# The first four weight units of a two-layer encoder: the order in which halves of the channels are multiplied, loaded and split

## The chip, the cores and the metric

The kernel runs on one core of one Trainium2 chip. The metric is the device time of the whole kernel in microseconds (us), lower is better. The engines are called PE (matrix multiply), DVE (vector), ACT (scalar), POOL (general purpose) and SP (which here only issues transfers).

## The reference

Two layers over a sequence of 256 tokens with 1024 channels. Each layer normalises x, multiplies it by one wide matrix W_in, feeds the columns of the product to three branches (grouped-query attention A, dilated window attention B, pooling C) and to gates, and ends with a SwiGLU mixer.

```python
for l in range(DEPTH):                       # DEPTH = 2
    h = rms_norm(x, norm_mix[l])             # x: 256 x 1024
    z = h @ w_in[l]                          # 1024 x 6656, 13 chunks of 512 columns
    qa, ka, va, qb, kb, vb, uc, gz = jnp.split(z, SPLIT_POINTS, axis=-1)
    qa = apply_axial_rope(rms_norm(qa...), ang_row, ang_col)
    ...
    x = x + merged @ w_out[l]
    h2 = rms_norm(x, norm_ffn[l])
    x = x + (jax.nn.silu(h2 @ w_ffn_gate[l]) * (h2 @ w_ffn_up[l])) @ w_ffn_down[l]
```

## The kernel before, in words

**Units.** All weights of a layer lie in the order of their use as 68 units of 128 x 2048 floats (1 MB): four tiles `k` of 128 channels by 512 output columns. A chunk z0 to z12 of W_in takes two units, one for each half of the channels. Before the change unit `t` holds chunk `t // 2`, half `t % 2`. Four slots (`RING`) hold the units; SP loads the next unit into a slot when PE has finished the one in it (`unit_done`).

**Products in three parts.** Products are made nearly exact by splitting both factors into a rounded part and a rest. For each unit ACT writes `w_hi`, a rounded copy of `w_raw` (L658, `split`), and DVE writes `w_lo = w_raw - w_hi` (L854). PE then runs, for each of the two token blocks m = 0, 1, the eight matmuls hi x hi and lo x hi of the four tiles (L1135, L1137) and the four with `w_lo` (L1146): 24 matmuls of 512 columns a unit. The first unit of a layer is split in four pieces, one for each tile (L654, L860), and in the first layer it is also loaded in four pieces.

**Turning x.** PE needs x with channels on the partitions. A "turn" `("mix_x", i)` is four transposes of 128 x 128 (L1168) of half `i // 2` of the channels and token block `i % 2` into a bank; DVE multiplies by the gains into `scratch` (L878), ACT writes the rounded part `aT_hi` (L670), and DVE the rest `aT_lo` (L887). Turns 0 and 1 are made ahead of a layer's first unit. Turns 2 and 3 are listed in `TURNS_WITHIN` at unit 0: PE transposes them between the eight `w_hi` matmuls and the four `w_lo` matmuls of block m = 0 (`TURNS_FIRST`). The norm itself is applied later: ACT squares x into sums (`x_squares`, L761), POOL turns the sums into `rstd` (`x_norms`), and ACT applies `rstd` when it takes a finished chunk out of its bank (`take_z`, L755 and L756).

**Programs.** Every engine has its own program, one stretch for each unit `t`, in which the order is written out by hand. ACT splits up to three units ahead in the first two stretches (`splits_at(t, ahead=3)`), DVE two. At the start of both layers ACT's order is: first unit, (first layer: turns,) units 1 and 2, (second layer: turns,) squares of both halves of x, unit 3, then z0. Once z0 is taken, DVE normalises and rotates heads (`rotate`, L929 to L953, then `norm_rotated`, L961) in stretches named in `REGIONS`, ACT cuts the heads into 16-bit halves (L730), SP transposes them by a transfer, and ACT joins them (`join_heads`, L736). The first scores (L1225) start ahead of unit 10 and wait for the join of region a_k. DVE's maximum over the scores is L967.

**Banks.** z0, z2 and z4 lie in banks 2 and 3, all other chunks of W_in in banks 0 and 1. So z6's first matmul of block 0, at unit 12, waits until ACT has taken block 0 of z5 (finished at unit 11).

**Start of the kernel.** SP issues, in this order: x's first half for m = 0, piece 0 of the first unit, x's first half for m = 1, pieces 1 to 3, x's second half (512 KB), units 1, 2 and 3. POOL issues its own loads (gains, rotary table, mask, biases) once x's second half has landed. PE runs warm-up matmuls (L1267) before and after the first two turns.

Of the kernel before, what the change touches and what calls it, by code (L numbers as in the profile page):

```python
# [16 lines left out]
F32 = mybir.dt.float32  # L17
# [3 lines left out]
ALU = mybir.AluOpType  # L21
# [3 lines left out]
P = 128  # L25
# [48 lines left out]
    ("a_q", QK_A_Q, 8, 0, 0, 0, (2, 3)),  # L74
    ("a_k", QK_A_K, 2, 8, 1, 1, (4, 4)),
# [8 lines left out]
JOINS_AHEAD = {8: [(1, 0), (1, 1)], 13: [(3, 0)]}  # L84
JOINS_BEHIND = {7: [(0, 0)], 10: [(0, 1)], 14: [(2, 0)], 15: [(4, 0)], 16: [(4, 1), (5, 0)], 17: [(3, 1)],
# [24 lines left out]
    0: [("mix_x", 2), ("mix_x", 3)],  # L110
# [8 lines left out]
TURNS_FIRST = (0, U_A1, U_OUT + 3, U_FFN)  # L119
# [24 lines left out]
def turns_within(t):  # L144
    return TURNS_WITHIN.get(t, [])
# [50 lines left out]
UNIT_ENDS = {(f"z{c}", 1): 2 * c + 1 for c in range(Z_CHUNKS)}  # L196
# [20 lines left out]
def splits_at(t, ahead=2):  # L217

    if t < 2:
        return {2: ([1], [2, 3]), 3: ([1, 2], [3])}[ahead][t]  # L220
    return [t + 2] if t + 2 < UNITS else []


def build(nc, x, stream, params, b_gate, eye, angles, pooling, mask, out):
# [3 lines left out]
    with ExitStack() as ctx:  # L228
# [3 lines left out]
        def sem(name):  # L232
            return ctx.enter_context(nc.semaphore(name))
# [86 lines left out]
        unit_landed = [sem(f"unit_landed{i}") for i in range(RING)]  # L320
        piece_landed = [sem(f"piece_landed{k}") for k in range(UK)]
# [67 lines left out]
        def wait_lo(eng, lay, name, former=False):  # L389

            n = SCALED_TURNS.index(name) + 1 + EARLY_TURNS - (len(SCALED_TURNS) if former else 0)
            eng.wait_ge(turn_lo, lay * len(SCALED_TURNS) + n)

# [71 lines left out]
        def _(sp):  # L465
# [8 lines left out]
            sp.sem_inc(unit_landed[0], 16)  # L474
            sp.dma_start(x_sb[:, :, NC:D], xv[:, :, NC:D]).then_inc(x1_loaded, 16)
# [165 lines left out]
        def _(act):  # L641
# [5 lines left out]
            def split_first(lay):  # L647

                if lay:
                    act.wait_ge(unit_landed[0], lay * (16 * UNITS // RING) + 16)  # L650
                for k in range(UK):
                    if lay == 0:
                        act.wait_ge(piece_landed[k], 16)
                    nc.scalar.activation(w_hi[:, 0, k, :], w_raw[:, 0, k, :], ACT.Copy).then_inc(first_hi, 1)  # L654
# [108 lines left out]


            act.wait_ge(half_ready, 1)
# [3 lines left out]
            turn(BEFORE, ("mix_x", 0))  # L769
            for lay in range(DEPTH):  # L770
                for t in range(UNITS):
                    for name in turns_before(t, lay):
                        turn(lay, name)
                    if t == 0:
                        split_first(lay)
                        if lay == 0:
                            turn(BEFORE, ("mix_x", 1))
                            for name in turns_within(t):
                                turn(lay, name)
                    for j in splits_at(t, ahead=3):  # L780
# [27 lines left out]
                    if t or lay:  # L808
                        for name in turns_within(t):
                            turn(lay, name)  # L810
                    if t == 0:
                        for half in range(2):
                            for m in range(MT):

                                b = X_BANKS[half] + m
                                act.wait_ge(bank_free[b], lay * USES[b] + 1)
                                if half == 1:
                                    act.wait_ge(x1_loaded, 16)
                                x_squares(lay, m, half)
                    if t % 2 == 1 and t // 2 <= POOL_CHUNK:  # L820
                        for m in range(MT):
                            if (t, m) != FIRST_OUT:
                                take_z(lay, t // 2, m)
# [15 lines left out]
        def _(dve):  # L839
# [11 lines left out]
            def split(lay, j):  # L851
                dve.wait_ge(unit_hi, lay * (UNITS - 1) + j)
# [3 lines left out]
            def split_first(lay):  # L856

                for k in range(UK):
                    dve.wait_ge(first_hi, lay * UK + (k + 1))
                    nc.vector.tensor_tensor(w_lo[:, 0, k, :], w_raw[:, 0, k, :], w_hi[:, 0, k, :].bitcast(F32),  # L860
                                            ALU.subtract).then_inc(first_lo, 1)
# [174 lines left out]
            for lay in range(DEPTH):  # L1036
# [3 lines left out]
                for t in range(UNITS):  # L1040
# [7 lines left out]
                    if t == 0:  # L1048
                        split_first(lay)
                        if lay == 0:  # L1050
                            low_turn(BEFORE, ("mix_x", 1))
# [66 lines left out]
        def _(pe):  # L1118
            pe.sem_inc(unit_done, RING)

            def rows(lay, t, name, m, src, tiles, wk, first, final, opening=False, ready=None):
# [8 lines left out]
                if opening and t:  # L1130
                    pe.wait_ge(unit_hi, lay * (UNITS - 1) + t)
                for i, k in enumerate(tiles):
                    if opening and not t:
                        pe.wait_ge(first_hi, lay * UK + (i + 1))
# [6 lines left out]
                if opening and t:  # L1141
                    pe.wait_ge(unit_lo, lay * (UNITS - 1) + t)
                for i, k in enumerate(tiles):
                    if opening and not t:
                        pe.wait_ge(first_lo, lay * UK + (i + 1))
                    last = nc.tensor.matmul(o, src[0][:, k, tok], w_lo[:, slot, wk + i, :], start=False,  # L1146
                                            stop=final and i == len(tiles) - 1)
                if final:
                    full(last, (name, m))
                return last  # L1150
# [127 lines left out]
            for lay in range(DEPTH):  # L1278
                for t in range(UNITS):
# [10 lines left out]
                    if t < U_C0:  # L1290
                        c, half = divmod(t, 2)
                        ready = (lambda m: wait_lo(pe, lay, ("mix_x", 2 * half + m), former=half == 0)) if c == 0 else None
# [81 lines left out]
def weight_stream(w_in, w_branch_a, w_branch_b, w_branch_c, w_out, w_ffn_gate, w_ffn_up, w_ffn_down):  # L1374
# [3 lines left out]
    for l in range(DEPTH):  # L1378
        u = units[l]
        w = w_in[l].reshape(2, UK, P, Z_CHUNKS, NC)  # L1380
        u[:U_C0] = w.transpose(3, 0, 2, 1, 4).reshape(2 * Z_CHUNKS, P, UK, NC)
        c = w_branch_c[l].reshape(UK, P, 2, NC)
# [55 lines left out]
```

## Time and profile before

| | |
|---|---|
| median of 3 runs | 810.91 us (810.03 to 812.22) |
| the profiled execution's own time | 810.14 us |
| its span, first to last instruction | 808.3 us |
| PE busy | 802.1 us, 3808 matmuls |
| DVE, ACT, POOL busy | 572.9, 464.0, 245.9 us |
| clock that PE was granted | full in every slice |

The span is what the trace covers; 1.84 us of the profiled execution's time lie around it. An engine's busy time says how much of the span it worked, not that it was waited for: a matmul's listed duration (0.39 us) is longer than the distance at which the next one starts (0.227 us), because matmuls overlap, so distances between starts are the better measure of PE.

### The profile page before, as it was taken

Reading aid. Unit: us, or ns where it says so; the run is one execution under the profiler, and the core shown is the slowest. Engines: PE = TensorE matmul, PEld = TensorE weight load, DVE = VectorE, ACT = ScalarE, POOL = GpSimd, SP = SyncE. Lnnn points to the kernel's source line nnn. Section 1 sums busy time; section 2 is a strip of 40 time slices with the busy share of each in tenths; the row PEclk is TensorE's granted clock in tenths of the full one; section 3 lists DMA queues with packets and bytes.
Section 4 is the critical chain, followed back from the end, with each engine's and each line's share of the span. In section 5 each row is a group of like instructions: output and inputs, shape, how many; then the busy total and the mean of one; then the engine's idle time right before and its main releaser. Section 6 shows DMA issues by size and latency. Waiting matters only on the chain.

```text
span 808.3 us, 9803 instructions
## 1 busy us (share of the span) xinstructions
PE 802.1 (99%) x3808; PEld 658.5 (81%) x3808; DVE 572.9 (71%) x684; ACT 464.0 (57%) x534; POOL 245.9 (30%) x206
## 2 busy tenths in 40 slices
PE   8999999999999999999999999999999999999998
PEld 6888877888888888888888887878888888888886
DVE  5899976758685666665379998777686666676551
ACT  5788886574355445544457888856635455355420
POOL 1342623330043444430023325342300444344200
PEclk9999999999999999999999999999999999999999
DMA  9788876864557787686456888675744666776651
GB/s 336 285 242 217 216 225 216 215 223 161 171 211 210 212 220 218 202 244 217 163 203 201 223 226 215 214 222 190 234 156 167 222 207 208 231 234 201 206 205 53
DMA packets 98318, 170.22 MB, mean 211 GB/s; under 512 B 78016, under 2 KB 78176, under 8 KB 80864
## 3 DMA queue, kind: packets, MB, share of 16 engines
q1 hardware_dynamic: 96352, 163.34, 65.5%
q0 software_dynamic: 1632, 6.18, 2.2%
q8 instruction: 30, 0.49, 0.2%
q14 instruction: 16, 0.13, 0.1%
q10 hardware_dynamic: 288, 0.08, 0.0%
HBM read 149.91 MB, written 1.05 MB: 187 GB/s over the span
## 4 chain that ended last, share of the span: by engine, by line
PE 97%; DVE 1%; DMA 1%; ACT 0%; SPq 0%; issue 0%
PE bank L1135 31%; PE bank L1146 30%; PE bank L1137 30%; PE bank L1257 2%; PE bank L1168 1%; PE bank L1234 1%; PE bank L1225 1%; PE bank L1195 1%; DMA x_sb<-in_x_dram 1%; PE bank L1201 0%; DVE w_lo L854 0%; DVE w_lo L860 0%; ACT w_hi L658 0%; DVE scratch L878 0%; DVE aT_lo L887 0%; ACT aT_hi L670 0%
## 5 line engine op out<-in xcount | busy, mean ns | idle before, releaser
L854 DVE TENSOR_TENSOR w_lo<-w_raw,w_hi 128x2048 fp32r<-128x2048 f32 x134 | 314.6, 2349 | 122.5 <-ACT w_hi L658 121.9
L658 ACT ACTIVATE w_hi<-w_raw 128x2048 fp32r<-128x2048 f32 x134 | 256.5, 1915 | 170.3 <-DMA w_raw<-in_stream_dram 170.3
L1135 PE MATMUL bank<-w_hi,aT_hi 128*128 128x512 f32 x832 | 327.6, 394 | 0.2 <-issue 0.2
L1137 PE MATMUL bank<-w_hi,aT_lo 128*128 128x512 f32 x832 | 324.1, 390 | 0.0
L1146 PE MATMUL bank<-w_lo,aT_hi 128*128 128x512 f32 x832 | 223.3, 390 | 0.2 <-DVE w_lo L854 0.2
L1135 PEld LDWEIGHTS bank<-w_hi,aT_hi 128*128 128x128 f32 x832 | 156.2, 188 | 36.6 <-issue 3.4
L1146 PEld LDWEIGHTS bank<-w_lo,aT_hi 128*128 128x128 f32 x832 | 155.6, 188 | 33.0 <-DVE w_lo L854 0.7
L1137 PEld LDWEIGHTS bank<-w_hi,aT_lo 128*128 128x128 f32 x832 | 156.3, 188 | 31.9
L597 POOL COPY halves<-hid 128x512 uint16<-128x512 uint16 x44 | 75.1, 1734 | 4.6 <-DVE hid L1107 4.6
L606 POOL COPY hT_raw<-turned 128x512 uint16<-128x512 uint16 x44 | 33.8, 813 | 134.4 <-DMA turned<-halves 134.4
L1135 PE MATMUL bank<-w_hi,hT_hi 128*128 128x512 f32 x176 | 68.6, 390 | 0.0
L1137 PE MATMUL bank<-w_hi,hT_lo 128*128 128x512 f32 x176 | 68.5, 389 | 0.0
L835 ACT ACTIVATE sg<-bank,rstd 128x256 f32<-128x256 f32 x44 | 20.9, 474 | 75.2 <-PE bank L1146 68.7
L556 POOL TENSOR_TENSOR sx<-ssx 128x2 f32<-128x2 f32 x4 | 4.0, 994 | 162.3 <-ACT probsT L761 162.3
L1146 PE MATMUL bank<-w_lo,hT_hi 128*128 128x512 f32 x176 | 47.7, 389 | 0.0
L1100 DVE SCALAR_TENSOR_TENSOR scratch<-bank,rstd,sg 128x256 f32<-128x256 f32 x44 | 21.1, 481 | 37.3 <-ACT sg L835 37.3
L1146 PEld LDWEIGHTS bank<-w_lo,hT_hi 128*128 128x128 f32 x176 | 33.0, 188 | 6.9
L1135 PEld LDWEIGHTS bank<-w_hi,hT_hi 128*128 128x128 f32 x176 | 33.0, 188 | 6.8
L1137 PEld LDWEIGHTS bank<-w_hi,hT_lo 128*128 128x128 f32 x176 | 33.1, 188 | 6.8
L552 POOL TENSOR_TENSOR rs<-rs_in,neg_half 128x8 f32<-128x8 f32 (+2 forms) x24 | 33.9, 1414 | 2.0
L550 POOL TENSOR_SCALAR rs_in<-ss 128x8 f32<-128x8 f32 (+2 forms) x24 | 8.2, 340 | 83.4 <-DVE ss L929 82.9
L1030 DVE TENSOR_TENSOR x_sb<-bank,x_sb 128x512 f32<-128x512 f32 x16 | 10.7, 686 | 28.3 <-PE bank L1146 28.1
(102 smaller groups left out, 801.6 us busy)
## 6 DMA issues: line engine op xcount, KB each, us to landing
w_raw<-in_stream_dram SPq DMA_DIRECT2D x135, 1024.0 KB, 5.2
bias_sb<-in_b_gate_dram POOLq DMA_DIRECT2D x12, 256.0 KB, 5.7
par<-in_params_dram POOLq DMA_DIRECT2D x3, 384.0 KB, 3.4
w_raw<-in_stream_dram SPq DMA_DIRECT2D x4, 256.0 KB, 5.0
pool_mat<-in_pooling_dram POOLq DMA_DIRECT2D x1, 1024.0 KB, 5.2
out_dram<-x_sb SPq DMA_DIRECT2D x4, 256.0 KB, 3.9
x_sb<-in_x_dram SPq DMA_DIRECT2D x2, 256.0 KB, 4.6
x_sb<-in_x_dram SPq DMA_DIRECT2D x1, 512.0 KB, 7.0
```

The lines of the kernel that those rows point to most:

```text
L552: nc.gpsimd.tensor_tensor(dst[0], dst[1], dst[2], ALU.pow).then_inc(signal, 1)
L597: nc.gpsimd.tensor_copy(halves[:, b, :, h, :], both[:, :, :, h]).then_inc(halves_ready, 1)
L606: nc.gpsimd.tensor_copy(both[:, :, :, :, h], turned[:, b, :, h, :, :].rearrange("p m k t -> p k m t")).then_inc(raw_ready, 1)
L658: nc.scalar.activation(w_hi[:, j % RING, :, :].rearrange("p k n -> p (k n)"), w_raw[:, j % RING, :, :].rearrange("p k n -> p (k n)"), ACT. ...
L835: nc.scalar.activation(sg[:, i % 2, m, :], B((f"f{i}", m))[:, 0:256], ACT.Sigmoid, scale=rstd[:, 1, m:m + 1]).then_inc(sig_done, 1)
L854: nc.vector.tensor_tensor(w[0], w[1], w[2].bitcast(F32), ALU.subtract).then_inc(unit_lo, 1)
L1030: free(nc.vector.tensor_tensor(part, B((name, m))[:, :], part, ALU.add), (name, m))
L1100: made.append(link(nc.vector.scalar_tensor_tensor(scratch[:, 2 * NC + 256 * m:2 * NC + 256 * m + 256], B((f"f{i}", m))[:, 0:256], rstd[:, ...
L1135: nc.tensor.matmul(o, src[0][:, k, tok], w_hi[:, slot, wk + i, :], start=first and i == 0, stop=False)
L1137: nc.tensor.matmul(o, src[1][:, k, tok], w_hi[:, slot, wk + i, :], start=False, stop=False)
L1146: last = nc.tensor.matmul(o, src[0][:, k, tok], w_lo[:, slot, wk + i, :], start=False, stop=final and i == len(tiles) - 1)
L1257: last = nc.tensor.matmul(B(("o", o))[HD * r:HD * r + HD, at:at + w], zvu[:, kt, col(r):col(r) + HD], joined_probs(2 * p + r)[:, c:c + cw] ...
```

## The change

The first four units of each layer change order: z0 half 0, z1 half 0, z0 half 1, z1 half 1. Hence z0 is finished after the third unit and z1, as before, after the fourth. In the first layer's load order the second unit, now in two halves of 512 KB, goes ahead of x's second half. The second unit is split in two pieces on ACT and DVE (`split_second`), and no unit is split further ahead in the first stretch; the squares of x's first half are made there, those of its second half between units 2 and 3. Turns 2 and 3 move from unit 0 to unit 1, and on ACT they stand ahead of unit 2's split. The first unit's matmuls get an order of their own (`first_unit`): `w_hi` products of both blocks piece by piece, all `w_lo` products last. At the kernel's start ACT splits piece 0 ahead of the first turn. Regions a_q and a_k are rotated one stretch later, and the joins of a_k stand behind unit 10's split and the cutting of heads.

```diff
-    ("a_q", QK_A_Q, 8, 0, 0, 0, (2, 3)),
-    ("a_k", QK_A_K, 2, 8, 1, 1, (4, 4)),
+    ("a_q", QK_A_Q, 8, 0, 0, 0, (3, 4)),
+    ("a_k", QK_A_K, 2, 8, 1, 1, (4, 5)),
...
-JOINS_AHEAD = {8: [(1, 0), (1, 1)], 13: [(3, 0)]}
+JOINS_AHEAD = {13: [(3, 0)]}
+JOINS_BEHIND = {7: [(0, 0)], 8: [(1, 0), (1, 1)], ...
...
-    0: [("mix_x", 2), ("mix_x", 3)],
+    1: [("mix_x", 2), ("mix_x", 3)],
...
-TURNS_FIRST = (0, U_A1, U_OUT + 3, U_FFN)
+TURNS_FIRST = (1, U_A1, U_OUT + 3, U_FFN)
+def z_unit(t):
+    return (t % 2, t // 2) if t < 4 else divmod(t, 2)
+def chunk_done(t):
+    return {2: 0, 3: 1}.get(t, t // 2 if t >= 5 and t % 2 else None)
...
-def splits_at(t, ahead=2):
+def splits_at(t):
     if t < 2:
-        return {2: ([1], [2, 3]), 3: ([1, 2], [3])}[ahead][t]
+        return ([], [2, 3])[t]
...
+            for h in range(2):
+                sp.dma_start(w_raw[:, 1, 2 * h:2 * h + 2, :]..., stream_v[...]).then_inc(second_landed[h], 16)
+            sp.sem_inc(unit_landed[1], 16)
             sp.dma_start(x_sb[:, :, NC:D], xv[:, :, NC:D]).then_inc(x1_loaded, 16)
-            for s in range(1, RING):
+            for s in range(2, RING):
...
+            split_piece(0, 0)
+            turn(BEFORE, ("mix_x", 0))
+            split_piece(0, 1)
+            turn(BEFORE, ("mix_x", 1))
             for lay in range(DEPTH):
...
                     if t == 0:
+                        for k in range(0 if lay else 2, UK):
+                            split_piece(lay, k)
+                        split_second(lay)
+                        squares_of_x(lay, 0)
+                    if t == 1:
+                        for name in turns_within(t):
+                            turn(lay, name)
+                    for j in splits_at(t):
                         split(lay, j)
+                        if t == 1 and j == 2:
+                            squares_of_x(lay, 1)
...
+            def first_unit(lay):
+                for m in range(MT):
+                    wait_free(pe, lay, ("z0", m))
+                wait_hi(pe, lay, ("mix_x", 0))
+                for pieces in ((0, 1), (2,), (3,)):
+                    for k in pieces:
+                        pe.wait_ge(first_hi, lay * UK + (k + 1))
+                        product(0, aT_hi, k, w_hi, k == 0)
+                    if pieces[0] == 0:
+                        wait_lo(pe, lay, ("mix_x", 0), former=True)
+                    for k in pieces:
+                        product(0, aT_lo, k, w_hi)
+                    if pieces[0] == 0:
+                        wait_hi(pe, lay, ("mix_x", 1))
+                    for k in pieces:
+                        product(1, aT_hi, k, w_hi, k == 0)
+                wait_lo(pe, lay, ("mix_x", 1), former=True)
+                for k in range(UK):
+                    product(1, aT_lo, k, w_hi)
+                for m in range(MT):
+                    for k in range(UK):
+                        if m == 0:
+                            pe.wait_ge(first_lo, lay * UK + (k + 1))
+                        last = product(m, aT_hi, k, w_lo)
```

## Rows read from the trace of the kernel before

**Rows 1.** The page: busy time of each engine, and the chain that ended last.
```profile
PE 802.1 (99%) x3808; PEld 658.5 (81%) x3808; DVE 572.9 (71%) x684; ACT 464.0 (57%) x534; POOL 245.9 (30%) x206
...
PE 97%; DVE 1%; DMA 1%; ACT 0%; SPq 0%; issue 0%
```

**Rows 2.** Timeline of PE, 0 to 22 us: start, duration, engine, line, operation.
```profile
6.97 1.39 PE L1267 MATMUL bank<-neg_half 128*68 128x68 f32 x20
8.56 0.47 PE L1135 MATMUL bank<-w_hi,aT_hi 128*128 128x512 f32 x1 [0.20 <-issue]
...
10.79 1.06 PE L1168 MATMUL bank<-ident,x_sb 128*128 128x128 f32 x8
...
17.59 1.21 PE L1146 MATMUL bank<-w_lo,aT_hi 128*128 128x512 f32 x4 [0.16 <-DVE w_lo L854]
...
21.39 0.39 PE L1135 MATMUL bank<-w_hi,aT_hi 128*128 128x512 f32 x1
```

**Rows 3.** Timeline of ACT and DVE over the same start.
```profile
7.39 1.66 ACT L654 ACTIVATE w_hi<-w_raw 128x512 fp32r<-128x512 f32 x3
...
13.31 1.90 ACT L658 ACTIVATE w_hi<-w_raw 128x2048 fp32r<-128x2048 f32 x1
...
15.24 2.29 DVE L854 TENSOR_TENSOR w_lo<-w_raw,w_hi 128x2048 fp32r<-128x2048 f32 x1 [1.11 <-ACT w_hi L658]
```

**Rows 4.** SP's issue of units 1 to 3, then each one's KB and us to landing.
```profile
4.33 1.77 SPq L477 DMA_DIRECT2D w_raw<-in_stream_dram  x3
...
w_raw<-in_stream_dram SPq DMA_DIRECT2D x1, 1024.0 KB, 8.7
...
w_raw<-in_stream_dram SPq DMA_DIRECT2D x1, 1024.0 KB, 11.1
...
w_raw<-in_stream_dram SPq DMA_DIRECT2D x1, 1024.0 KB, 14.2
```

**Rows 5.** Timeline, 407 to 421 us: the start of the second layer.
```profile
409.40 1.03 PE L1168 MATMUL bank<-ident,x_sb 128*128 128x128 f32 x8
...
410.80 1.28 DVE L878 TENSOR_TENSOR scratch<-bank,par 128x512 f32<-128x512 f32 x2
...
411.51 1.24 ACT L670 ACTIVATE aT_hi<-scratch 128x512 fp32r<-128x512 f32 x2 [2.39 <-DVE scratch L878]
...
419.50 0.39 PE L1135 MATMUL bank<-w_hi,aT_hi 128*128 128x512 f32 x1
...
420.69 0.69 ACT L755 ACTIVATE gates<-bank,rstd 128x512 f32<-128x512 f32 x1 [3.68 <-POOL rstd L552]
```

**Rows 6.** Busy time of each engine in a window (us, instructions, clock, DMA).
```profile
30.00:67.00 37.00, 37.00 (x172) 30.26 (x170) 36.38 (x60) 29.81 (x43) 15.12 (x18) 1.00 0.78 234
```

**Rows 7.** Timeline of DVE: ends of its unbroken stretch in either layer.
```profile
24.48 0.28 DVE L911 TENSOR_TENSOR rope<-rope_c,par 128x128 f32<-128x128 f32 x1
...
67.44 1.28 DVE L967 TENSOR_REDUCE neg_max<-bank 128x2 f32<-128x512 f32 x2
...
424.95 2.29 DVE L854 TENSOR_TENSOR w_lo<-w_raw,w_hi 128x2048 fp32r<-128x2048 f32 x1 [2.98 <-ACT w_hi L658]
...
465.16 1.28 DVE L967 TENSOR_REDUCE neg_max<-bank 128x2 f32<-128x512 f32 x2
```

**Rows 8.** Timeline of ACT: a join of heads, and the last z5 reads.
```profile
57.60 0.84 ACT L736 ACTIVATE qkT<-zqk 128x256 uint16<-128x256 uint16 x2
...
75.87 0.67 ACT L756 ACTIVATE zvu<-bank,rstd 128x512 f32<-128x512 f32 x1
...
473.77 0.71 ACT L756 ACTIVATE zvu<-bank,rstd 128x512 f32<-128x512 f32 x1
```

**Rows 9.** Timeline of PE: first scores, and unit 12 in both layers.
```profile
65.00 1.35 PE L1225 MATMUL bank<-qkT 64*128 64x256 f32 x10
...
77.98 0.39 PE L1135 MATMUL bank<-w_hi,aT_hi 128*128 128x512 f32 x1
...
476.09 0.39 PE L1135 MATMUL bank<-w_hi,aT_hi 128*128 128x512 f32 x1
```

More of the change, by code:

```diff
@@ L320, in build @@
         unit_landed = [sem(f"unit_landed{i}") for i in range(RING)]
+        second_landed = [sem(f"second_landed{h}") for h in range(2)]
+        second_hi = sem("second_hi")
+        second_lo = sem("second_lo")
         piece_landed = [sem(f"piece_landed{k}") for k in range(UK)]
@@ L807, in _ @@
                                                  ACT.Sigmoid).then_inc(gate_done, 1)
-                    if t or lay:
+                    if t != 1:
                         for name in turns_within(t):
                             turn(lay, name)
[L811 to L820, printed above, removed]
+                    if chunk_done(t) is not None and chunk_done(t) <= POOL_CHUNK:
                         for m in range(MT):
                             if (t, m) != FIRST_OUT:
-                                take_z(lay, t // 2, m)
+                                take_z(lay, chunk_done(t), m)
                     if t in (U_OUT + 3, U_FFN):
@@ L1129, in rows @@
                     ready(m)
-                if opening and t:
-                    pe.wait_ge(unit_hi, lay * (UNITS - 1) + t)
+                if opening and t > 1:
+                    pe.wait_ge(unit_hi, lay * (UNITS - 2) + (t - 1))
                 for i, k in enumerate(tiles):
-                    if opening and not t:
-                        pe.wait_ge(first_hi, lay * UK + (i + 1))
+                    if opening and t == 1 and i % 2 == 0:
+                        pe.wait_ge(second_hi, lay * 2 + (i // 2 + 1))
                     nc.tensor.matmul(o, src[0][:, k, tok], w_hi[:, slot, wk + i, :], start=first and i == 0,
@@ L1149, in rows, with product @@
                     full(last, (name, m))
+                return last
+            def first_unit(lay):
+                def product(m, src, k, w, opens=False):
+                    return nc.tensor.matmul(B(("z0", m))[:, :], src[:, k, P * m:P * m + P], w[:, 0, k, :],
+                                            start=opens, stop=False)
+                for m in range(MT):
[16 more added lines that the diff above has]
+                    product(1, aT_lo, k, w_hi)
+                for m in range(MT):
+                    for k in range(UK):
+                        if m == 0:
+                            pe.wait_ge(first_lo, lay * UK + (k + 1))
+                        last = product(m, aT_hi, k, w_lo)
                 return last
@@ L1289, in _ @@
                         values(lay, 2 * q + 1)
-                    if t < U_C0:
-                        c, half = divmod(t, 2)
-                        ready = (lambda m: wait_lo(pe, lay, ("mix_x", 2 * half + m), former=half == 0)) if c == 0 else None
+                    if t == 0:
+                        last = first_unit(lay)
+                    elif t < U_C0:
+                        c, half = z_unit(t)
+                        ready = (lambda m: wait_lo(pe, lay, ("mix_x", 2 + m))) if t == 2 else None
                         last = columns(lay, t, f"z{c}", aT, range(UK * half, UK * half + UK), half == 0, half == 1,
@@ L1381, in weight_stream @@
         u[:U_C0] = w.transpose(3, 0, 2, 1, 4).reshape(2 * Z_CHUNKS, P, UK, NC)
+        u[[1, 2]] = u[[2, 1]]
         c = w_branch_c[l].reshape(UK, P, 2, NC)
```

71 lines of the change are left out of this document (44 added, 27 removed).

## The prediction

> **What bounds the kernel now.** I read the page first: PE is busy 99% of the span and the chain that ended last is 97% PE [rows 1]. So the time is the sum of PE's matmuls plus the few stretches in which PE doesn't start one every 0.227 us. The change has as many matmuls as before, so only such stretches, and the moment of the first matmul, can move the time. For these I read PE's timeline. At the kernel's start the first product begins at 8.56 and unit 2 at 21.39 [rows 2]. That is 12.83 us for 48 matmuls (2 units of 24) at 0.227 us, 10.88 us, and 8 transposes, 0.79 us: 11.67 us of work and 1.16 us idle. One wait of it is named, for `w_lo` of unit 1 at 17.59; others are for pieces of the first unit. At the start of the second layer the transposes begin at 409.40, eight matmuls after the layer's first, so the layer begins at 407.59, and unit 2 begins at 419.50 [rows 5]: 11.91 us for the same 11.67 us, 0.24 us idle. The most that these places can give is thus 1.40 us, and an earlier first matmul. A kernel of 811 us can't be told from no change within 0.3%, 2.4 us.
>
> Then I asked who runs close behind PE. DVE is busy 36.38 of the 37 us from 30 to 67 [rows 6], one unbroken stretch from the rotary tables to the maximum over the first scores [rows 7]. Whatever delays its beginning delays its end.
>
> **First layer, up to unit 2.** The second group of warm-up matmuls ends at 8.36, and the first product was held to 8.56 by `aT_lo`, which lies in "issue" [rows 2]. `first_unit` begins with hi x hi and needs neither. Piece 0 is split before 6.85, when ACT turns to x, so the bound is the warm-up: start 8.30, a gain of 0.26 us. Pieces come from ACT every 0.55 us from 7.39 on (three in 1.66) [rows 3], the last about 10.0. By then only 8 of its 24 matmuls are through, and the new order has 16 to run before the first `w_lo`, at 11.9; DVE, which needs 0.6 us a piece, has them by 11.5. Unit 0 runs without a gap and ends at 8.30 + 5.44 = 13.74.
>
> Unit 1's data: it landed at 4.33 + 8.7 = 13.03, behind x's second half [rows 4]. Ahead of it, its halves land near 10.7 and 11.9 and x's second half where unit 1 did, 13.0. Both of ACT's half splits cost between 0.95 (half of 1.90) and 1.1 (two pieces) [rows 3]; with 1.05 they end at 11.75 and 13.0. DVE's halves, between 1.15 and 1.3 each, end at 14.2. PE needs the first at 13.74, the lows at 16.3. All hidden. The one extra start on ACT and on DVE is hidden with them; without that cover it would be 0.15 to 0.3 us.
>
> **The new wait.** Call A the start of the transposes of turns 2 and 3, now after unit 1's first eight matmuls: A = 13.74 + 1.81 = 15.55. DVE can begin once the first four are done: between A + 0.40 (half the transposes) and A + 1.40, the distance from 409.40 to 410.80 [rows 5], at which DVE was still busy with other work. I take A + 0.70, nearer to the first. ACT begins the turn 0.71 later (410.80 to 411.51) and needs 1.24 for two [rows 5], so ACT is free at A + 2.65. Only now does unit 2's split stand in its program, 1.90 us [rows 3]: A + 4.56. Before, it was done ahead of the turns. DVE's part, 2.29 us [rows 3], ends at A + 6.88. PE meanwhile does the transposes (0.79) and 16 matmuls (3.63) and wants unit 2's `w_hi` at A + 4.42: it waits 0.18 us. It wants `w_lo` eight matmuls later, A + 6.41, and gets it at A + 6.93: 0.52 us. Behind it nothing is lost twice: unit 3's split follows the squares (two of a piece's size, 0.6 each), ends at A + 7.7, and is wanted at A + 10.5. New wait: 0.70 us in each layer, between 0 (if ACT's and DVE's steps overlap by 0.7 us more) and 1.2 (0.5 us added for semaphores).
>
> First layer: unit 2 would start at 8.30 + 11.67 + 0.18, its `w_lo` stall included 20.67, against 21.39: **-0.72 us**. Second layer: the 0.24 idle goes, 0.70 comes: **+0.45 us**. The split into halves costs nothing there, as unit 1's data is there long before.
>
> **DVE's and ACT's lag.** x's sums end later. First layer: ACT ends unit 3's split at A + 7.7 = 23.25, DVE's part ends at 25.5, and the unbroken stretch begins there instead of at 24.48, 1.05 us late [rows 7]. z0 (unit 4's split and four steps of ACT, by 28.0) is then not what DVE waits for. So the maxima, the exponentials behind them and ACT's read of z5, block 0, come 1.05 us later: 75.87 + 0.67 + 1.05 = 77.6 [rows 8]. PE wants that bank at 77.98 - 0.72 = 77.3 for unit 12 [rows 9]: **+0.3 us**. Second layer: POOL takes long over `rstd` here: ACT was free of unit 3's split 3.68 us before 420.69 and had ended the squares one split earlier, 420.69 - 3.68 - 1.90 = 415.11, so 5.58 us [rows 5]. Now the squares end at A + 5.8 with A = 407.59 + 7.25 = 414.84, so `rstd` comes at 426.2; ACT then takes both blocks of z0 (four steps of 0.57 to 0.69, to 428.5) and splits unit 5, to 430.4. DVE is through with unit 3 (424.8) and the rotary tables (2 us) at 426.7, starts its stretch there instead of at 424.95 [rows 7], and waits about 1.5 us for that split: 3.1 us late at the maxima. z5, block 0, is read by 473.77 + 0.71 + 3.1 = 477.6, wanted at 476.09 + 0.45 = 476.5 [rows 8, 9]: 1.0 us, of which I take **+0.9**, since ACT's short idles in between take up some. Block 1 of z5 is finished 12 matmuls, 2.7 us, after block 0, so behind that read ACT has time to catch up and the lag isn't passed on. Bounds of this term: 0, and twice the value.
>
> **Sum.** -0.72 + 0.45 + 0.3 + 0.9 = +0.9 us on the span of 808.3: 809.2, and with the 1.84 us around it 811.1 for the profiled execution, which took 810.14. The median of the runs is 0.77 us above that execution, so I give 811.8.
>
> **Other waits I priced.** The joins of a_k ended at 58.44, 6.6 us ahead of the scores at 65.00 [rows 8, 9]. With a_k a stretch later, behind unit 10's split (1.9) and one cutting (1.0), I get 61.7 against 64.3, in the second layer about 1.9 us of room. POOL's loads start 2.4 us later; the gains and rotary table are wanted 1 us later too.
>
> A rule of the Trainium skill bears on unit 2's landing. The rows: unit 2 landed near 16.0, 3.0 us behind unit 1, while POOL's loads were under way [rows 4]; unchanged, it has 2 us before ACT wants it at 18.2. "DMA: Bandwidth & Descriptors", section on queues, rings and completion order, says that each engine takes turns between its queues packet by packet; an even share with POOL's loads would make unit 2 take twice unit 1's 2.4 us and land at 17.8. By the row there is no wait and by the rule just none. It is why a late unit 2 is a rival below.
>
> **Rivals.** (1) The waits don't come: ACT and DVE overlap their steps, z5 is read in time. Then 1.40 and 0.26 us are gained: 809.2, still no change that can be told. For it: three pieces on ACT take 1.66 us together [rows 3], so each starts before the listed end of the one before. Against: ACT's order, which puts the turns ahead of the split. Chance 0.2. (2) Slower: DVE's stretch. In the second layer it has 1.9 us of room at the joins and 2.6 us at unit 9's `w_lo`. If each of its region steps starts later for waiting on ACT's splits, by over 1.9 us more than my 3.1, the scores stop PE and z5's read too: each further us is paid once, and above 2.4 us in all the kernel is slower by 0.3%, 813.4 to 814.5. For it: the lag already uses most of the room. Chance 0.11. (3) Unit 2 or x's second half lands over 2 us late: PE waits at its most expensive place; 1 us late beyond the room gives 812.8. Chance 0.04. My forecast: 0.65.
>
> **Numbers.** Low end 809.2, from rival 1; high end 813.5, where the z5 term is doubled (+1.2) and each layer's new wait is halfway to its upper bound (+0.5 in all). Faster than 808.5 needs more idle time than there is: 0.03. Slower than 813.3: 0.12. Within: 0.85.
>
> **What would show it.** First product at 8.3; no idle in unit 0; a wait of PE on `w_lo` of unit 2 near 22 and near 421; unit 2 begun near 20.2 and 419.5; DVE's maxima 1 and 3 us later; a late start of unit 12 near 477. I'm wrong if these waits are missing, or if PE waits at the scores or for unit 9.

## The result, and the profile after

The changed kernel takes 812.89 us (median of 11 runs, 811.94 to 813.95) against 810.91 us (11 runs, 809.94 to 812.22): 1.0025 times as long, 95% interval 1.0016 to 1.0034. It is 2 us slower, within the 0.3% called no change; 811.8 was forecast. The profiled execution took 812.89 us with a span of 811.1 us. The page of the kernel after, busy times and the chain that ended last:

```profile
PE 804.5 (99%) x3808; PEld 660.1 (81%) x3808; DVE 575.8 (71%) x686; ACT 463.9 (57%) x536; POOL 241.0 (30%) x206
...
PE 90%; DVE 4%; ACT 2%; issue 2%; DMA 1%; SPq 0%; DVEq 0%; ACTq 0%
```

PE was 97% of that chain [rows 1] and is 90% now: it has been handed over to DVE and ACT in more places. The list of PE's waits after (us in total, times, longest) is short:

```profile
PE bank L1246 <- DMA ident<-in_eye_dram: 1.0, 1, 1.0
PE bank L1345 <- POOL neg_half L561: 0.9, 1, 0.9
PE bank L1182 <- ACT zvu L787: 0.7, 1, 0.7
PE bank L1193 <- DVE w_lo L892: 0.3, 2, 0.2
```

The list counts only idle time between listed durations, so a wait covered by a matmul's long listed tail is nearly invisible. I therefore also took the start of every unit's first matmul from the timelines and compared distances. From unit 2's start to unit 3's it takes 5.44 us in before, 24 matmuls of 0.227 us. The rows below are one profile of each kernel; the second numbers of before and after, in the first and the last column, are from their second profiles (before_again and again). The names of the other rows are those of the experiments below. In us, second layer behind the comma:

| | first product | units 0–1, layers 1, 2 | unit 2, layers 1, 2 | units 10–11 | units 12–13 | first product to end |
|---|---|---|---|---|---|---|
| before | 8.56, 8.87 | 12.83, 11.92 | 5.44, 5.44 | 11.05, 11.05 | 12.90, 12.90 | 799.8, 799.8 |
| after | 9.64, 9.17 | 11.93, 11.80 | 5.98, 6.04 | 11.22, 11.24 | 13.04, 13.84 | 801.4, 801.6 |
| split2_first | 9.34 | 11.88, 11.78 | 5.44, 5.44 | 11.27, 11.23 | 13.07, 15.14 | 801.5 |
| z6_banks | 9.94 | 12.05, 11.80 | 5.99, 6.00 | 11.06, 11.05 | 12.89, 12.90 | 800.4 |
| x_ahead | 9.21 | 12.70, 11.80 | 6.00, 6.02 | 11.27, 11.25 | 13.07, 14.78 | 803.2 |
| regions_old | 8.59 | 11.97, 11.80 | 5.99, 6.00 | 11.13, 11.06 | 13.03, 13.28 | 800.6 |
| regions_split2 | 9.31 | 11.90, 11.80 | 5.44, 5.44 | 11.06, 11.06 | 12.90, 12.90 | 798.8 |
| all_three | 10.06 | 12.24, 11.81 | 5.44, 5.44 | 11.05, 11.05 | 12.90, 12.90 | 799.5 |
| before_third | 8.39 | 13.01, 11.91 | 5.44, 5.44 | 11.05, 11.05 | 12.90, 13.91 | 800.9 |
| before_warm18 | 10.02 | 12.67, 11.89 | 5.44, 5.44 | 11.05, 11.39 | 12.90, 13.07 | 800.2 |
| after_warm18 | 8.56 | 11.90, 11.81 | 6.04, 5.99 | 11.34, 11.26 | 13.03, 14.04 | 802.1 |
| best_warm18 | 8.00 | 12.25, 11.81 | 5.73, 5.44 | 11.05, 11.05 | 12.90, 12.90 | 799.4 |

From before to after, in order: the first product 1.08 later; units 0–1 0.90 shorter; unit 2 0.54 longer; units 10 to 13 0.31 longer. Second layer: 0.12 shorter, 0.60 longer, and 1.13 longer at units 10 to 13. That is 2.64 of the 2.7 us that the span grew.

**The new wait at unit 2.** Timeline of the kernel after, first layer: PE, ACT and DVE from the moved transposes on. It answers to [rows 2, 3].

```profile
17.03 1.03 PE L1246 MATMUL bank<-ident,x_sb 128*128 128x128 f32 x8
...
17.66 1.29 DVE L923 TENSOR_TENSOR scratch<-bank,par 128x512 f32<-128x512 f32 x2 [2.90 <-PE bank L1246]
18.39 1.23 ACT L701 ACTIVATE aT_hi<-scratch 128x512 fp32r<-128x512 f32 x2 [3.65 <-DVE scratch L923]
19.52 1.90 ACT L689 ACTIVATE w_hi<-w_raw 128x2048 fp32r<-128x2048 f32 x1
...
21.45 2.29 DVE L892 TENSOR_TENSOR w_lo<-w_raw,w_hi 128x2048 fp32r<-128x2048 f32 x1 [1.11 <-ACT w_hi L689]
21.57 0.47 PE L1182 MATMUL bank<-w_hi,aT_hi 128*128 128x512 f32 x1
...
23.80 1.20 PE L1193 MATMUL bank<-w_lo,aT_hi 128*128 128x512 f32 x4 [0.15 <-DVE w_lo L892]
```

ACT is idle 3.65 us ahead of the turn, and unit 2's split, whose data is there, stands behind it. PE wants `w_lo` 1.81 us (8 matmuls of 0.227) after 21.57, at 23.38, and gets it at 23.80. The second layer has the same chain: transposes at 415.87, unit 2 at 420.41, `w_lo` at 422.65.

### The profile page after: what moved, and what is told of

The parts are those of the page before. It is cut to its first block, busy times and chain, and to the rows that moved or that the text cites. A ratio compares the mean times of both kernels' runs of the same rounds, so it can differ in the third digit from the quotient of the medians.

```text
span 811.1 us, 9809 instructions
## 1 busy us (share of the span) xinstructions
PE 804.5 (99%) x3808; PEld 660.1 (81%) x3808; DVE 575.8 (71%) x686; ACT 463.9 (57%) x536; POOL 241.0 (30%) x206
## 3 DMA queue, kind: packets, MB, share of 16 engines
HBM read 149.91 MB, written 1.05 MB: 186 GB/s over the span
## 4 chain that ended last, share of the span: by engine, by line
PE 90%; DVE 4%; ACT 2%; issue 2%; DMA 1%; SPq 0%; DVEq 0%; ACTq 0%
PE bank L1182 28%; PE bank L1193 27%; PE bank L1184 27%; PE bank L1335 2%; PE bank L1202 1%; PE bank L1246 1%; DVE w_lo L892 1%; PE bank L1312 1%; ACT w_hi L689 1%; DMA w_raw<-in_stream_dram 1%; PE bank L1273 1%; DMA x_sb<-in_x_dram 1%; DVE zqk L993 1%; DVE scratch L989 1%; DVE zqk L1006 0%
## 5 line engine op out<-in xcount | busy, mean ns | idle before, releaser
L689 ACT ACTIVATE w_hi<-w_raw 128x2048 fp32r<-128x2048 f32 x132 | 252.5, 1914 | 162.4 <-DMA w_raw<-in_stream_dram 162.4
L1182 PE MATMUL bank<-w_hi,aT_hi 128*128 128x512 f32 x816 | 321.4, 394 | 0.8 <-ACT zvu L787 0.7
L1184 PE MATMUL bank<-w_hi,aT_lo 128*128 128x512 f32 x816 | 317.9, 390 | 0.0
L1193 PE MATMUL bank<-w_lo,aT_hi 128*128 128x512 f32 x816 | 219.1, 390 | 0.3 <-DVE w_lo L892 0.3
L1182 PEld LDWEIGHTS bank<-w_hi,aT_hi 128*128 128x128 f32 x816 | 153.2, 188 | 37.2 <-issue 3.0
L1193 PEld LDWEIGHTS bank<-w_lo,aT_hi 128*128 128x128 f32 x816 | 152.6, 188 | 32.6 <-DVE w_lo L892 1.2
L1184 PEld LDWEIGHTS bank<-w_hi,aT_lo 128*128 128x128 f32 x816 | 153.2, 188 | 31.3
```

The source lines that it names most:

```text
L689: nc.scalar.activation(w_hi[:, j % RING, :, :].rearrange("p k n -> p (k n)"), w_raw[:, j % RING, :, :].rearrange("p k n -> p (k n)"), ACT. ...
```

## The experiments

Each ratio is to the kernel before, run alongside on the same chip; medians are of 10 or 11 runs (x_ahead: 6; before_again and before_third are one run each). The bracket behind a ratio is its 95% interval.

**again: the changed kernel as it is.**

> The changed kernel unaltered, to see what of its trace comes back. Theory: its losses are fixed waits (PE on w_lo of unit 2 in both layers, the bank waits at unit 12 in both layers and at unit 14 in the second), so they come back at the same places with the same sizes, and it is 1.5 to 2.2 us slower than before. The late first product (9.64 us after the span's start, 8.56 before) is chance: the instructions up to there are the same in both kernels but for ACT's order, so in this trace it may as well lie at 8.3 to 8.6. Rival: the late start belongs to the change, because the first product needs something that comes later; then it lies at 9.6 again.

Measured: 812.71 us, 1.0032 [1.0021, 1.0042], span 810.8. Every wait came again: unit 2 takes 6.00 us in both layers, units 10–11 11.25 and 11.27, units 12–13 13.03 and 14.10. The loss is real, and so is its place.

**split2_first: ACT's split of unit 2 back ahead of the turns.**

```diff
-                    if t == 1:
-                        for name in turns_within(t):
-                            turn(lay, name)
                     for j in splits_at(t):
                         split(lay, j)
                         if t == 1 and j == 2:
+                            for name in turns_within(t):
+                                turn(lay, name)
                             squares_of_x(lay, 1)
```

> ACT splits unit 2 ahead of turns 2 and 3 instead of behind them, nothing else. Theory: the wait of PE at unit 2 comes from this order alone. It should go in both layers (about 0.5 us each), the squares of x's second half and unit 3's split end 1.9 us sooner, so DVE's unbroken stretch begins sooner and the waits at units 12 (0.3 and 0.3 us) and 14 (0.8 us) go as well: 2.0 to 2.5 us below the changed kernel, 0 to 0.5 us below the kernel before. Rival A: the wait at unit 2 is due to DVE's chain of turn and w_lo; then a wait of 0.2 to 0.5 us stays at unit 2. Rival B: the waits at 12 and 14 come from z0 being complete one unit later, whatever ACT's order; then they stay and only about 1 us is won.

Measured: 812.04 us, 1.0014 [1.0005, 1.0022], span 810.9. Unit 2 is back at 5.44 us in both layers, so ACT's order is the whole cause of that wait. Unit 1 takes 6.34 us here and 6.36 in after. Units 10 to 13 keep their delay, and the wait of unit 14 in the second layer, 0.8 in after, is 2.0 us here. So in the profiled execution nothing is won, and over the medians 0.7 us. PE's timeline in this kernel, from 489 us on (the first row is cut off by that window):

```profile
488.67 0.81 PE L1302 MATMUL bank<-qkT 64*128 64x256 f32 x6
491.48 0.50 PE L1181 MATMUL bank<-w_hi,aT_hi 128*128 128x512 f32 x1 [2.00 <-ACT zvu L787]
```

**z6_banks: z6 in banks 2 and 3, so that it doesn't wait for z5's read.**

```diff
-        pair(2 if c in (0, 2, 4) else 0, f"z{c}")
+        pair(2 if c in (0, 2, 4, 6) else 0, f"z{c}")
```

> Chunk z6 is collected in banks 2 and 3 instead of 0 and 1, behind z4. So z6 at unit 12 doesn't wait for the read of z5, nor z7 at unit 14 for the read of z6. Theory: the waits at units 12 and 14 are waits for banks; they go (0.3, 0.3 and 0.8 us, 1.4 us in all) and those at unit 2 stay, so 1.2 to 1.5 us below the changed kernel and 0.4 to 0.8 us above the kernel before. Rival: behind them lies w_hi or w_lo coming late; then PE stops at units 12 to 14 all the same and less than 0.5 us is won.

Measured: 811.66 us, 1.0009 [1.0000, 1.0017], span 810.3. Units 10 to 13 are at before's 11.05 and 12.9 in both layers, and unit 2 keeps its 0.6 us. The maxima are as late as in after. What the lag costs is thus paid at the banks of z6 and z7, and only there.

**x_ahead: x's second half loaded ahead of the second unit again.**

```diff
+            sp.dma_start(x_sb[:, :, NC:D], xv[:, :, NC:D]).then_inc(x1_loaded, 16)
             for h in range(2):
                 sp.dma_start(w_raw[:, 1, 2 * h:2 * h + 2, :]..., stream_v[...]).then_inc(second_landed[h], 16)
             sp.sem_inc(unit_landed[1], 16)
-            sp.dma_start(x_sb[:, :, NC:D], xv[:, :, NC:D]).then_inc(x1_loaded, 16)
```

> x's second half is issued ahead of the second unit's two halves again, the rest of the change stays. Theory: the order of these loads is worth nothing: the halves land about 1.3 us later (12.5 and 13.7), their last split ends near 14.8 against a need at 15.4 for w_hi and 17 for w_lo if the first product lies at 8.3 to 8.6 and later if not; at most 0.3 us is lost, and POOL's loads come 2.4 us sooner. Within 0.3 us of the changed kernel. Rival: the order is what lets unit 1 follow unit 0; then PE waits 0.5 to 1 us at unit 1 and the kernel is that much slower than the changed one.

Measured: 813.68 us, 1.0032 [1.0020, 1.0043], the ratio of "again"; span 812.4. From unit 1's first matmul to unit 2's it is 6.36 us, as in after. The profiled execution's units 0–1 are 0.8 us longer, but that lies in unit 0, under a lower clock (below). The load order is worth nothing that this can tell.

**regions_old: a_q and a_k rotated, and a_k joined, where they were.**

```diff
-    ("a_q", QK_A_Q, 8, 0, 0, 0, (3, 4)),
-    ("a_k", QK_A_K, 2, 8, 1, 1, (4, 5)),
+    ("a_q", QK_A_Q, 8, 0, 0, 0, (2, 3)),
+    ("a_k", QK_A_K, 2, 8, 1, 1, (4, 4)),
...
-JOINS_AHEAD = {13: [(3, 0)]}
-JOINS_BEHIND = {7: [(0, 0)], 8: [(1, 0), (1, 1)], 10: ...
+JOINS_AHEAD = {8: [(1, 0), (1, 1)], 13: [(3, 0)]}
+JOINS_BEHIND = {7: [(0, 0)], 10: ...
```

> The changed kernel with one part undone: a_q and a_k are rotated, cut and joined in the stretches of before (a_q at 2 and 3, a_k at 4). In the four traces of the changed order, DVE's first maxima begin 2.1 us behind unit 10's first matmul, and 0.1 us in the kernel before, whatever ACT's order at unit 2. Theory: DVE idles while it waits for the split of unit 6 and has one rotation of 2.7 us more behind it, because a_q's blocks stand one stretch later. With the old stretches the maxima come 0 to 1 us behind unit 10, the waits at units 12 (0.3 us in each layer) and 14 (0.8 to 2.1 us in the second) go, those at unit 2 stay: 1.3 to 1.8 us below the changed kernel. Rival: the lag comes from z0 being complete one unit later, which this doesn't alter; then the maxima stay 2 us behind and nothing is won.

Measured: 812.22 us, 1.0011 [1.0003, 1.0020], span 809.2. Units 10–11 wait 0.08 and 0.01 us; units 12–13 wait 0.13 us in the first layer and 0.38 in the second, of which the list of waits puts 0.3 on unit 14; unit 2 keeps its 0.6. From the first product to the end it takes 0.8 us less than after.

**regions_split2: both edits together.**

> The old stretches for a_q and a_k, and ACT's split of unit 2 ahead of turns 2 and 3. Theory: all waits that the change brought are gone (unit 2 in both layers 1.1 us, unit 12 0.6 us, unit 14 0.8 to 2.1 us), its gains at the first two units stay: 2.5 to 3 us below the changed kernel, 0.2 to 0.8 us below the kernel before. Rival: the first product of the changed kernel begins later than that of before by more than chance; then it ends within 0.3 us of before or above it.

Measured: 810.55 us, 0.9995 [0.9986, 1.0004], span 808.1. Every distance behind unit 2 is before's, and from the first product to the end it takes 1.0 us less than before (798.8 against 799.8). The median doesn't show that, since the first product is 0.75 us later.

**all_three: these two and z6's banks.**

> As the one with old stretches and unit 2 split first, and z6 in banks 2 and 3 besides. Theory: with the lag gone the banks aren't waited for, so this adds nothing: within 0.3 us of it. Rival: some lag stays and the banks are still worth 0.3 us or more.

Measured: 810.25 us, 0.9990 [0.9981, 0.9999], span 809.5 with a first product at 10.06. The third edit adds nothing once the lag is gone.

**before_again and before_third: the kernel before, one profile each.**

> The kernel before, unaltered, for a second look at its start. Theory: the clock of PE in the first 10 us is chance, not the change: the distance between the first transposes may as well be 0.23 us here as 0.13, and the first product lie at 9.2 to 9.9 instead of 8.56. Rival: the kernel before always begins at 8.5 to 8.6, and the late start belongs to the change.

> The kernel before, unaltered, for a third look at its start. So far its first product lay at 8.56 and 8.87 us after the span's start, that of the changed order and its variants at 8.59 in one trace and 9.17 to 10.06 in seven. Theory: chance, the instructions of PE up to there are the same; a third look may be early or late. Rival: it belongs to the change; then 8.5 to 8.9 again.

Measured: 810.53 us (first product 8.87) and 811.11 us (8.39). Before's early start is no single lucky profile. The third profile shows something else: unit 14 waits 1.0 us in the second layer, without any lag (below).

**before_warm18, after_warm18, best_warm18: 18 warm-up matmuls ahead of the first transposes instead of 14** in before, in after and in all_three.

```diff
-WARM_BANK, WARM_LOADS, WARM_SPLITS = 1, 14, 10
+WARM_BANK, WARM_LOADS, WARM_SPLITS = 1, 18, 10
```

> The kernel before with 18 warm-up matmuls ahead of the first turn instead of 14, so that PE has work until the first loads land at 5.0 to 5.6 us instead of being idle from 4.3. Theory: the late starts come of that idle second; the kernel before begins early mostly, so it gains little: 0 to 0.4 us below before. Rival: the four matmuls more delay the first turn and nothing is gained: 0 to 0.3 us above.

> The changed kernel with 18 instead of 14 warm-up matmuls. Theory: its transposes then follow at 0.13 us instead of 0.23 and its first product lies at 8.3 to 8.6 instead of 9.2 to 9.9; it ends 0.6 to 1.1 us below the changed kernel, 0.9 to 1.5 us above before. Rival: the slow stretch isn't set by the idle second; then 9.2 to 9.9 again and no gain.

> The variant with old stretches of a_q and a_k, unit 2 split first and z6 in banks 2 and 3, with 18 instead of 14 warm-up matmuls. Theory: it keeps the changed order's 1 us at the first two units and begins early: 1.2 to 1.8 us below the kernel before. Rival: the start stays late, and it is 0.6 to 0.9 us below before, as without the added warm-ups.

Measured: before 810.63 us, 0.9999 [0.9990, 1.0008], first product 10.02; after 812.27 us, 1.0018 [1.0009, 1.0027], first product 8.56; all_three 809.40 us (809.16 to 810.92), 0.9981 [0.9972, 0.9990], first product 8.00, span 807.4. That last one beats both kernels, by 1.5 us below before; its interval lies apart from 1. Before's kernel can start late too, so a late start isn't a property of the changed order alone. More warm-up gives before nothing; the intervals of after and of all_three with 14 and with 18 overlap, so it isn't shown to give them anything either.

best_warm18 also shows what an earlier start is worth. Its first product is 1.31 us earlier than in regions_split2, yet from there to the end it takes 0.6 us longer (799.4 against 798.8). The losses are at the start: units 0–1 take 12.25 instead of 11.90 us, where PE stands 0.33 us in the middle of unit 0 (the last piece lands at 9.67 and ACT splits it at 9.70), and unit 2 takes 5.73 instead of 5.44. So the forecast that unit 0 runs without a gap holds at a start of 8.56 (after_warm18, 5.55 us for unit 0) and no longer at 8.00 (5.91 us).

## Why the prediction was right, and where it wasn't

**The first product: wrong, by 1.3 us.** 8.30 was forecast, 9.64 came. PE is slow there, in work that stands ahead of the first unit. PE's timeline of the kernel after, then of best_warm18:

```profile
5.34 2.34 PE L1246 MATMUL bank<-ident,x_sb 128*128 128x128 f32 x8 [0.97 <-DMA ident<-in_eye_dram]
7.47 2.37 PE L1345 MATMUL bank<-neg_half 128*68 128x68 f32 x20
9.64 0.47 PE L1202 MATMUL bank<-w_hi,aT_hi 128*128 128x512 f32 x1
```

```profile
5.10 0.66 PE L1245 MATMUL bank<-ident,x_sb 128*128 128x128 f32 x4
6.30 0.66 PE L1245 MATMUL bank<-ident,x_sb 128*128 128x128 f32 x4 [0.55 <-DMA x_sb<-in_x_dram]
6.80 1.39 PE L1344 MATMUL bank<-neg_half 128*68 128x68 f32 x20
8.00 0.71 PE L1201 MATMUL bank<-w_hi,aT_hi 128*128 128x512 f32 x2
```

The same twenty warm-ups take 2.37 us in one and 1.39 in the other, and before had 1.39 [rows 2]. The product begins as they end. Where PE is quick, the step holds: with `first_unit` the product begins 1.20 us behind the first of the twenty warm-ups (6.80 to 8.00 in best_warm18, 7.36 to 8.56 in after_warm18, 7.39 to 8.59 in regions_old), and in the three profiles of before 1.59 to 1.62 us behind it. So the order gains 0.39 us where 0.26 was forecast, and the slow PE takes more than that away. Late starts came in 7 of 8 profiles of the changed kernel and its variants at 14 warm-ups (9.17 to 10.06, and once 8.59) and in none of 3 of before (8.39 to 8.87). Whether the changed order makes them more frequent stays open: the operations of PE ahead of its first product are the same in both, and before_warm18 started at 10.02.

**Units 0 and 1: right in size, with one term wrong.** 11.67 us of work and a wait of 0.18 us for unit 2's `w_hi` were forecast, 11.85 in all; 11.93 and 11.80 came, against 12.83 and 11.92 before: 0.90 and 0.12 us gained, where 0.98 and 0.06 were forecast. But the wait didn't occur. `w_hi` is ready at 21.42 (19.52 + 1.90), and PE begins unit 2 at 21.57, 0.91 us behind the start of the last four matmuls of unit 1, which is their full pace. And in split2_first, where that `w_hi` is ready well ahead, unit 1 takes as long (6.34 against 6.36 us). The work was put 0.13 us too low instead: unit 1 takes 6.36 us for 24 matmuls and eight transposes (5.44 + 0.79), and 0.10 of the rest lie in the first four matmuls behind the transposes, 1.01 us (17.82 to 18.83) for 0.91. Unit 1's halves landed at 11.21 and 12.43 (10.7 and 11.9 forecast) and took ACT 1.06 us each (1.05 forecast):

```profile
11.23 1.06 ACT L684 ACTIVATE w_hi<-w_raw 128x1024 fp32r<-128x1024 f32 x1 [1.12 <-DMA w_raw<-in_stream_dram]
12.45 1.06 ACT L684 ACTIVATE w_hi<-w_raw 128x1024 fp32r<-128x1024 f32 x1 [0.16 <-DMA w_raw<-in_stream_dram]
```

**The new wait at `w_lo`: right.** With A at 17.03, DVE begins at A + 0.63 (0.70 forecast), ACT's turn at A + 1.36 (1.41), unit 2's split at A + 2.49 (2.65) and ends at A + 4.39 (4.56); DVE's part ends at A + 6.71 (6.88). Of the 0.70 us forecast for a layer, the 0.18 ahead of unit 2 didn't come (above); for the other 0.52, at `w_lo`, 0.54 and 0.60 were measured. split2_first removed them and changed nothing else near by: this cause is shown.

**Unit 2's landing: rival 3 didn't happen.** The row for the issue of units 2 and 3 in after (SP issues both from 5.46 on; min, median, max us to landing):

```profile
L499 SPq DMA_DIRECT2D w_raw<-in_stream_dram x2: 597/684/770, 5.5 to 6.3; - x2
...
DMA to landing us min/median/max: 10.7/12.5/14.3
```

Unit 2 landed near 16.2, 2.5 us behind x's second half (4.75 + 9.0), and ACT wanted it at 19.52. Unit 3 landed near 20.6, 4.4 us behind unit 2. By the rule in the Trainium skill, "DMA: Bandwidth & Descriptors", section on queues, rings and completion order, each DMA engine takes turns between its queues packet by packet; the prediction's estimate from it was a landing at 17.8. The trace sides with the row for unit 2, since POOL's loads were issued only at 14.0. Unit 3 was under way together with them: its 4.4 us, for what took unit 2 2.5, look like an even share, and in six more of the ten profiles with the changed order it took 4.3 to 4.9 us. But in the other three (regions_old, split2_first, best_warm18), with POOL's loads issued at the same time, it took 2.9. The profiles don't settle the rule.

**DVE's lag: right in the first layer; in the second too large, and from another cause.** Lag here means the distance from unit 10's first matmul to the first maximum over the scores. Before: 0.51 and 0.12 us. After: 2.07 and 2.09. The forecast had it grow by 1.77 us in the first layer (maxima 1.05 later, PE 0.72 earlier) and by 2.65 in the second (3.1 less 0.45); it grew by 1.56 and 1.97. The first maximum itself is 2.3 and 3.5 us later than before, of which 0.7 and 1.5 us are PE's own delay up to there.

In the first layer the forecast chain is the one that runs. DVE's timeline of the kernel after:

```profile
24.48 2.29 DVE L892 TENSOR_TENSOR w_lo<-w_raw,w_hi 128x2048 fp32r<-128x2048 f32 x1 [0.74 <-ACT w_hi L689]
```

It is unit 3's part, begun late because ACT splits unit 3 behind unit 2 and the squares. From 24.48 DVE has no idle of 0.1 us up to the maximum at 69.73: 45.25 us of work, while PE reaches unit 10 in 43.2. In before the same work took 45.17 us, from 22.27.

In the second layer it isn't that start. DVE at unit 6's part and at the maximum in after, where unit 10 begins at 466.55:

```profile
435.54 2.29 DVE L892 TENSOR_TENSOR w_lo<-w_raw,w_hi 128x2048 fp32r<-128x2048 f32 x1 [0.78 <-ACT w_hi L689]
...
468.64 1.28 DVE L1012 TENSOR_REDUCE neg_max<-bank 128x2 f32<-128x512 f32 x2
```

Then split2_first, with unit 10 at 465.11:

```profile
434.10 2.29 DVE L891 TENSOR_TENSOR w_lo<-w_raw,w_hi 128x2048 fp32r<-128x2048 f32 x1 [0.78 <-ACT w_hi L689]
```

DVE stands there 0.78 us for ACT's split of unit 6. ACT makes that split behind its read of z1's second block, for which it waits on PE, so it keeps its place in PE's order. From that start to the maximum DVE works 33.1 us without a break, and PE reaches unit 10 in 31.0: the difference is the lag of 2.1 us. It is the same in the second layer of all six profiles with the new stretches, whatever came ahead, and in split2_first in the first layer too. In before, unit 6's part begins without idle at 435.39 and the maximum follows 29.8 us later. The 3.3 us more are one block of a_q, rotated and normalised behind unit 6 instead of ahead of it. Hence split2_first alone didn't shorten the lag.

With the old stretches the late start sets the lag again: in regions_old DVE's unbroken work begins with unit 3's part at 422.23. The first maximum in regions_old (unit 10 at 465.41) and then in regions_split2 (464.73):

```profile
466.55 1.28 DVE L1012 TENSOR_REDUCE neg_max<-bank 128x2 f32<-128x512 f32 x2
```

```profile
464.62 1.28 DVE L1011 TENSOR_REDUCE neg_max<-bank 128x2 f32<-128x512 f32 x2
```

So in the second layer the lag halves (1.14) and goes (-0.11); in the first it stays at 1.98 in regions_old and is 1.05 in regions_split2. Not every lag costs time: before_again has 1.48 in its first layer, where unit 3 landed late (21.63, 19.70 in before), and PE waits for nothing.

Of the forecast's terms for the second layer `rstd` was wrong as well: it is ready at 423.7, not 426.2, because POOL's three operations take 2.2 us from 421.57, where 5.58 was counted from the end of the squares. The wait of z6 that follows was forecast at 0.3 and 0.9 us. Measured over units 10 to 13, without unit 14's: 0.31 and about 0.33. That the lag grew by 0.68 us less than forecast fits the missing 0.57 in the second layer.

**The step that failed: "behind that read ACT has time to catch up and the lag isn't passed on".** It is passed on, not through ACT's work but through SP's program and a weight load. Timeline of SP and ACT in after, 476 to 491 us:

```profile
476.24 2.58 SPq L520 DMA_TRANSPOSE gates<-scratch  x2
478.87 0.58 SPq L534 DMA_DIRECT2D w_raw<-in_stream_dram  x1
...
485.98 1.92 ACT L689 ACTIVATE w_hi<-w_raw 128x2048 fp32r<-128x2048 f32 x1 [2.92 <-DMA w_raw<-in_stream_dram]
487.81 1.35 ACT L767 ACTIVATE qkT<-zqk 128x1024 uint16<-128x1024 uint16 x1
489.02 1.98 ACT L752 ACTIVATE scratch<-probs 128x1024 uint16<-128x1024 uint16 x2
490.90 1.25 ACT L787 ACTIVATE zvu<-bank,rstd 128x512 f32<-128x512 f32 x2
```

The same in before:

```profile
472.98 3.00 SPq L498 DMA_TRANSPOSE gates<-scratch  x2
476.28 0.33 SPq L512 DMA_DIRECT2D w_raw<-in_stream_dram  x1
...
487.47 1.24 ACT L756 ACTIVATE zvu<-bank,rstd 128x512 f32<-128x512 f32 x2
```

The probabilities come later from ACT, so SP is held at their transposes until 478.8 instead of 476.0. Behind them in its program stands the load of unit 15's weights, issued 2.6 us later and landed 485.96 instead of 482.52. ACT sits idle for it 2.92 us, and its read of z6 comes at 490.90 instead of 487.47. Unit 14 (z7) wants z6's bank and begins 0.8 us late. Without the lag (regions_split2) the load is issued at 475.98, and the wait is gone; with half the lag it is issued at 476.77, and the wait is 0.3 us; without z7's need of that bank (z6_banks) the load is as late, 479.25, and nothing waits. So the wait runs over this load: this much is shown. Of the 2.6 us, though, only a part is SP's. The load can't be issued before PE has finished unit 11, and PE is 1.7 us later there (477.79 against 476.09 for unit 12's start). Counted from unit 12's start, the load is issued 0.19 us behind it in before and 1.08 in after: the transposes hold it up by 0.9 us. The rest is the load itself, 7.1 us from issue to landing instead of 6.2. Both are needed. Counted the same way, it lands 6.4 us behind unit 12's start in before and 8.2 in after. In all seven profiles in which unit 14 waits for ACT it begins 5.66 to 5.68 us behind this landing; unit 14 isn't due before 12.90 us behind unit 12's start, so a landing up to 7.2 costs nothing. before_warm18 shows that limit: its load is issued 1.09 us behind, takes 6.1 and lands at 7.15, and unit 14 doesn't wait. So SP's hold uses up the margin of 0.8 us, and the slower load makes the wait.

The load's time isn't steady: over the fourteen profiles the same 1 MB took 5.2 to 8.4 us, 7.1 to 8.4 in the seven with a lag of over 1 us in the second layer, 5.2 to 6.2 in six of the seven others. Unit 14's wait is 0.8 to 2.0 us in kernels with the full lag. before_third, with its load issued at 476.27 as in before but landed at 484.3, waits 1.0 us too; it is the seventh of those others, with 8.05 us. Whether the lag makes the load slower, and how, isn't shown; chance alone can do it.

**The sum.** Forecast +0.9 us on the span, measured +2.7. Of the 1.8 us missed, 1.3 are the first product, and 0.8 unit 14; the other errors are under 0.6 and cancel in part. The range and the forecast of "no change, slightly slower" held, and the sum of the terms behind the first product (+1.2 forecast without its 0.26) compares with +1.6 measured. That sum is partly luck: the z5 term of the second layer was 0.57 us too large and hid most of the 0.8 us at unit 14 that had been put at nothing. Rival 1 is refuted by unit 2's wait, rival 2 in its form too: neither the scores nor unit 9's `w_lo` stopped PE.

## What to carry to other kernels

When one engine is busy 99% of the time, follow the slots that set the others' order: an operation put ahead of ready work on ACT costs PE its whole length less the slack, here 0.6 us a layer. A lag on a helper engine is paid wherever a bank or a queue is handed over. Follow it through the queues too, since a transfer that waits for late data holds back every load issued behind it. Moving rotations a stretch later to suit a late chunk cost 2.7 us from the first product to the end once the split stood in front (801.5 against 798.8, one profile each), and the late chunk alone made PE wait nowhere (regions_split2): leave such a follow-up edit out until the trace asks for it.

## What was not expected of the hardware

Eight transposes and twenty warm-ups at the kernel's start take 2.34 and 2.37 us in after, where best_warm18 needs 1.32 (twice 0.66) and 1.39. The moment at which PE turns to the longer durations varies: in x_ahead and all_three the first four transposes still take 0.66 us, and the warm-ups 2.25 and 2.47; in before_third it is the other way round, 1.12 us for the first four transposes, then 0.66 for the next four and 1.39 for the warm-ups. The granted clock doesn't always tell it. Busy times in windows of the start of after (us; PE, PEld, DVE, ACT, POOL, granted clock, DMA share, GB/s):

```profile
5.30:7.40 2.10, 1.95 (x8) 1.56 (x9) 0.69 (x1) 0.73 (x2) 0.00 (x0) 1.00 1.05 370
7.40:8.50 1.10, 1.10 (x12) 1.10 (x11) 0.78 (x2) 1.10 (x3) 0.00 (x0) 1.00 0.89 248
```

The same view of all_three:

```profile
7.00:8.50 1.50, 1.41 (x10) 1.41 (x11) 0.75 (x2) 1.14 (x2) 0.00 (x0) 0.61 0.88 210
8.50:10.00 1.50, 1.50 (x16) 1.50 (x16) 1.50 (x4) 1.16 (x3) 0.00 (x0) 0.50 0.92 279
```

In after the row says full clock, 2.4 GHz, while these operations take 1.7 times as long; in all_three it says 0.50, the level of 1.2 GHz, from 8.5 to 10.0 us, and in x_ahead from 7.5 to 10.75. PE had been idle 1.0 us ahead of the first transposes in after and 1.6 in all_three, waiting for `ident`, but before had idled 1.0 us as well. What decides stays open.

POOL's three operations for `rstd` in the second layer take 0.44, 2.11 and 2.64 us in all three profiles of before, 1.07, 0.19 and 0.71 in after and in the variants that keep its order on ACT, and 1.7, 2.3 and 0.78 in those that split unit 2 ahead of the turns, with the same shapes. So the durations go with ACT's order; why wasn't tried.
